# First weights whole with five loads in flight, and layer three's across product and mean of squares one unit later

## What is computed

```python
def hybrid_layer(x, mem, w_in, ...):              # layers one and two
    a_q, a_k, ..., m_q, m_z = split(x @ w_in)
    y_a = chunk_band_attention(...)               # 8 heads
    o_b = gla_chunk_recurrence(...)               # 4 heads, linear attention
    o_b = o_b * rsqrt(mean(square(o_b)) + RMS_EPS) * gla_norm_g
    mk, mv = split(mem @ w_mem_kv)
    y_m = memory_attention(m_q, mk, mv)           # 4 heads
    y = concat([y_a * silu(a_z), y_b * silu(b_z), y_m * silu(m_z)])
    return layer_norm(ALPHA * x + y @ w_out)

def second_block(x, ...):                         # layer three
    proj = rms_norm(x) @ w_in
    y_a = hgrn2_mixer(q, f, i, g)                 # 8 heads, linear attention, mean of squares per head
    y_b = fox_mixer(q, k, v, f_logit)             # 8 heads, causal softmax with decay
    merged = sigmoid(g_a) * (y_a @ w_up_a) + sigmoid(g_b) * (y_b @ w_up_b)
    x = x + rms_norm(merged @ w_o)
    gate, up = split(rms_norm(x) @ w_ffn_in)
    return x + rms_norm((silu(gate) * up) @ w_ffn_down)
```

## Time and profile before

| | us |
|---|---|
| median of three runs | 2255.04 (2253.93 to 2255.54) |
| the profiled execution's own time | 2254.65 |
| its span | 2252.8 |
| PE busy | 2241.2, 99% of the span |
| DVE busy | 1551.6, 69% |
| ACT busy | 1296.8, 58% |
| DMA | 460.04 MB, mean 204 GB/s |
| granted TensorE clock, mean | 0.999 |

### The profile page before, as it was taken

One profiled execution on the slowest core, in us unless ns is written; L12 is line 12 of the kernel. 1 busy time (PEld: TensorE's weight loads), 2 busy tenths in 40 slices (PEclk: granted clock), 3 DMA queues, 4 the chain that ended last, 5 costly groups with the idle time before them and its releaser, 6 DMA issues.

```text
span 2252.8 us, 35130 instructions
## 1 busy us (share of the span) xinstructions
PE 2241.2 (99%) x14045; PEld 2014.6 (89%) x14045; DVE 1551.6 (69%) x1756; ACT 1296.8 (58%) x1740; POOL 12.8 (1%) x18
## 2 busy tenths in 40 slices
PE   9999999999999999999999999999999999999998
PEld 8899998888999988889998999988999999998887
DVE  6576577775766777788787577866766766665555
ACT  6445576454555764666765467555655556554444
POOL 0000000000000000000000000000000000000000
PEclk9999999999999999999999999999999999999999
DMA  9655558676545684666565656685666666667664
GB/s 329 209 164 173 174 181 280 230 234 202 168 153 187 190 298 152 222 190 195 186 197 184 186 173 197 203 296 189 200 205 200 195 205 205 197 224 242 202 203 148
DMA packets 130532, 460.04 MB, mean 204 GB/s; under 512 B 13848, under 2 KB 20544, under 8 KB 128448
## 3 DMA queue, kind: packets, MB, share of 16 engines
q1 hardware_dynamic: 129376, 451.43, 61.9%
q0 software_dynamic: 848, 6.30, 0.8%
q10 hardware_dynamic: 144, 0.07, 0.0%
HBM read 449.35 MB, written 8.40 MB: 203 GB/s over the span
## 4 chain that ended last, share of the span: by engine, by line
PE 98%; DVE 1%; ACT 1%; DMA 0%; issue 0%; SPq 0%; DVEq 0%; ACTq 0%
PE banks L317 93%; PE banks L417 1%; PE banks L402 1%; PE banks L446 1%; PE banks L381 1%; PE banks L409 1%; DMA early<-in_kv_t 0%; DVE wl L650 0%; ACT wh L483 0%; PE banks L461 0%; PE banks L460 0%; PE banks L459 0%; PE banks L425 0%; DVE b L828 0%; DVE x_buf L923 0%
## 5 line engine op out<-in xcount | busy, mean ns | idle before, releaser
L650 DVE TENSOR_TENSOR wl<-raw,wh 128x1024 fp32r<-128x1024 f32 x774 | 941.1, 1223 | 476.9 <-ACT wh L483 474.5
L483 ACT ACTIVATE wh<-raw 128x1024 fp32r<-128x1024 f32 (+1 forms) x777 | 813.4, 1052 | 500.4 <-PE banks L317 437.2
L317 PE MATMUL banks<-xx,wh 128*128 128x512 f32 (+1 forms) x3760 | 858.5, 380 | 0.0
L317 PEld LDWEIGHTS banks<-xx,wh 128*128 128x128 f32 (+1 forms) x3760 | 688.2, 189 | 91.9 <-issue 1.0
L317 PEld LDWEIGHTS banks<-xx,wl 128*128 128x128 f32 x3712 | 455.2, 192 | 13.6
L317 PE MATMUL banks<-xx,wl 128*128 128x256 f32 x3712 | 464.6, 276 | 0.0
L317 PE MATMUL banks<-wh,xx 128*128 128x512 f32 x1504 | 360.2, 380 | 0.0
L317 PEld LDWEIGHTS banks<-wh,xx 128*128 128x128 f32 x1504 | 282.7, 189 | 39.4
L317 PE MATMUL banks<-wl,xx 128*128 128x512 f32 x752 | 196.1, 379 | 0.0
L317 PEld LDWEIGHTS banks<-wl,xx 128*128 128x128 f32 x752 | 142.1, 189 | 20.1
L317 PE MATMUL banks<-wh,yy 128*128 128x512 f32 x416 | 98.4, 379 | 0.0
(11 more groups left out here) (280 smaller groups left out, 1759.0 us busy)
## 6 DMA issues: line engine op xcount, KB each, us to landing
raw<-in_w_in_f SPq DMA_DIRECT2D x304, 512.0 KB, 3.6
raw<-in_w_ffn_f SPq DMA_DIRECT2D x160, 512.0 KB, 4.0
raw<-in_w_ffn_down SPq DMA_DIRECT2D x88, 512.0 KB, 4.3
raw<-in_w_in_t SPq DMA_DIRECT2D x80, 512.0 KB, 3.7
raw<-in_w_out_t SPq DMA_DIRECT2D x64, 512.0 KB, 4.8
raw<-in_w_o_t SPq DMA_DIRECT2D x32, 512.0 KB, 4.6
raw<-in_kv_f SPq DMA_DIRECT2D x16, 512.0 KB, 4.1
raw<-in_w_up_a_f SPq DMA_DIRECT2D x16, 512.0 KB, 3.5
```

Source lines behind the costliest of these rows:

```text
L317: return self.e.matmul(bank, stationary, moving, start=start, stop=stop, skip_group_check=True)
L483: self.e.activation(hi, source, ACT.Copy).then_inc(done.sem, 1)
L650: self.e.tensor_tensor(lo, source, hi.bitcast(f32), ALU.subtract).then_inc(done.sem, 1)
```

## The change

Three things are changed. The first weight is one unit again, the six `early` buffers are gone, and five loads are sent at the start; a load after that waits for its buffer's unit. In layer three the across product is written one unit later, and in all layers the mean of squares is. The mean of squares reads its columns in turn, and the root puts them back in order.

```diff
-        NR, NH, NE, AHEAD = 5, 4, 6, 2
+        NR, NH, AHEAD = 5, 4, 2
...
-        l_raw = lines(*(f"l_raw{n}" for n in range(NR + NE)))
+        l_raw = lines(*(f"l_raw{n}" for n in range(NR)))
...
-                    self.e.matmul(banks[6 + i], mean_r[:, :], a.hi[:, c], start=True, stop=False)
-                    j = self.e.matmul(banks[6 + i], mean_r[:, :], a.lo[:, c], start=False, stop=True)
+                    self.e.matmul(banks[6 + i], mean_r[:, :], in_turn(a.hi[:, c]), start=True, stop=False)
+                    j = self.e.matmul(banks[6 + i], mean_r[:, :], in_turn(a.lo[:, c]), start=False, stop=True)
...
-                    self.e.activation(r, banks[6 + i], ACT.Ln, bias=a.eps).then_inc(logged[i].sem, 1)
+                    self.e.activation(by_half(r), in_order(banks[6 + i]), ACT.Ln, bias=a.eps).then_inc(logged[i].sem, 1)
...
-                if early:
-                    plan(*among.pop(0))
-                    for kk in range(2):
-                        plan(w[0, :, 512 * kk:512 * kk + 512])
-                for u in range(early, n):
+                for u in range(n):
...
-            early = [at(f"early{n}", 48 + 4 * n, 1024) for n in range(NE)]
...
-                free = cut[n - NR] if n >= NE + NR else ()
-                sent.append(load(line, dst, src, *free))
+                free = cut[n - NR] if n >= NR else ()
+                sent.append(load(l_raw[n % NR], dst, src, *free))
...
-                if early:
-                    among_tok.append(cut[take(1)])
-                    for kk in range(2):
-                        unit_t(take(1), [(pr[t], act, t, kk, 0, kk == 0, False) for t in range(2)], among_tok[-1])
-                for k0 in range(2 * early, nk - 8 if late else nk, 2):
+                for k0 in range(0, nk - 8 if late else nk, 2):
...
                 if not a.both:
                     yield
+                    yield
                 tok = after(leveled)
                 x.across_halves(a, d, bank_free[6] + bank_free[7], tok)
...
                 x.split_squares(a, (sq[1], tok), h, l)
+                yield
                 yield
                 tok = after(meaned)
                 x.mean_squares(a, (h, l, co[1], t_exact), (), tok)
...
-            for n in range(NE + NR):
+            for n in range(NR):
                 send(n)
```

More of the change, by code:

```diff
@@ L1075, in send @@
                     return
-                src, (dst, line) = units[n][0], raw_of(n)
-                dst = dst[:, :]
+                src, dst = units[n][0], raw[n % NR][:, :]
                 if units[n][1] == "narrow":
@@ L1081, in send @@
                     dst = dst[:, 0:S * src.shape[1]].rearrange("p (a b) -> p a b", a=src.shape[1])
-                dst = dst[:, 0:src.shape[1]] if len(src.shape) == 2 else dst
-                free = cut[n - NR] if n >= NE + NR else ()
-                sent.append(load(line, dst, src, *free))
+                free = cut[n - NR] if n >= NR else ()
+                sent.append(load(l_raw[n % NR], dst, src, *free))
                 if n == 28:
@@ L1090, in split @@
                 src, hi, lo, free = units[n]
-                r = raw_of(n)[0][:, :]
+                r = raw[n % NR][:, :]
                 narrow = hi == "narrow"
@@ L1097, in split @@
                     hi, lo = place[n][0][:, :], place[n][1][:, :]
-                    if not narrow:
-                        hi, lo, r = (v[:, 0:src.shape[1]] for v in (hi, lo, r))
                 first, wide = hi, r
@@ L1225, in cols_t @@
                 ready = tuple(free) + bank_free[pr[0]] + bank_free[pr[1]]
-                early = among == "early"
-                if early:
-                    among_tok.append(cut[take(1)])
-                    for kk in range(2):
-                        unit_t(take(1), [(pr[t], act, t, kk, 0, kk == 0, False) for t in range(2)], among_tok[-1])
-                for k0 in range(2 * early, nk - 8 if late else nk, 2):
-                    if among and (k0 % 4 == 0 or early and k0 == 2):
+                for k0 in range(0, nk - 8 if late else nk, 2):
+                    if among and (k0 % 4 == 0 or among == "early" and k0 == 2):
                         among_tok.append(cut[take()])
```

## The result

| | before | after |
|---|---|---|
| median, the two measured together | 2254.01 (2253.46 to 2255.54, 11 runs) | 2259.56 (2258.31 to 2260.52, 11 runs) |
| ratio, 95% interval | | 1.0024 (1.0016 to 1.0031) |
| the profiled execution's own time | 2254.65 | 2259.41 |
| its span | 2252.8 | 2257.6 |
| granted TensorE clock, mean | 0.999 | 0.998 |

The changed kernel is 5.55 us slower, 0.25%. That is inside the range of the prediction, but not its likeliest case: it is a little over the 4.5 us that bound "no change" (the interval has the 0.2% in it, so on which side it lies is not settled), and, as the next rows show, it is the rival in which the clock falls.

A forecast was written before the change was run, and what follows sets the result against it. PE, busy 99% of 2252.8 us, was taken to bound the kernel. Start +0.1, across product -0.36, columns in turn -0.28 and mean of squares +4.1 summed to +3.56: median 2258.6 us, range 2256.2 to 2261.5.

The forecast's parts named there:

- likeliest case: Whole kernel: median 2258.6 us, 0.16% up and inside the 0.2% counted as no change; chance 0.55.
- the rival in which the clock falls: PE's new 4.7 us wait in layer three: clock drops, warm-up costs 1.9 us more, 2260.5 us; chance 0.22.
- The bound: Whole kernel: PE is busy 99% of 2252.8 us; moving waits could win under 3 us.
- Start, +0.1: First weight whole, five loads: second weight ready about as before; cost +0.1 us, bounds -0.1 and +0.5.
- The rival that rested on that stand: Start: PE idle 5.36 to 7.43, first weight's products at 1.2 GHz, 2.5 us lost, 2261.1 us; chance 0.11.
- Across product, -0.36: Layer three, first head group: one unit later covers DVE's product and removes PE's wait at L425; -0.36 us.
- In turn, -0.28: Sixteen mean-of-squares products: 0.215 us each instead of 0.233 when columns are read in turn; -0.28 us, bounds 0 and -0.3.
- Levels, 0: Layer three's level products (L446): no PE wait appears after the shift; 0 us, bounds -0.1 and +0.5.
- The stand, +4.1: Layer three, second group's mean of squares (L468): PE stands 4.68 us, old stall goes; net +4.1, bounds +3.6 and +4.5.
- PEclk whole in the slice of 1215 to 1235: Sign for the forecast: PE's granted clock stays full around its new wait at L468 in layer three.
- The sum: Whole kernel: 0.1 - 0.36 - 0.28 + 4.1 = +3.56 us, giving profile 2258.2 and median 2258.6.

The follow-up runs named there:

- e1: Kernel before with only the new start (first weight whole, five loads in flight): 2254.35 us, ratio 0.9999.
- e4: Kernel before with only the two added units (across product and mean of squares one unit later): 2260.21 us, ratio 1.0026.
- e6: Kernel before with only the across product of layer three's first group one unit later: 2258.56 us, ratio 1.0019.
- e10: Kernel before with only the columns of the mean of squares read in turn: 2254.23 us, ratio 1.0001.
- e3: Kernel before with five loads in flight at the start, first weight still in halves: 2254.48 us, ratio 1.0002.
- e5: Changed kernel with 19 unused products of the constant matrix on PE while it waits for the last mean of squares: 2257.37 us, ratio 1.0012.
- e8: Changed kernel whose walk no longer runs the lane to its end ahead of the second softmax group: 2252.57 us, ratio 0.9993.
- e9: Changed kernel with 8 unused products of the constant matrix on PE before the last mean of squares: 2257.67 us, ratio 1.0017.

## Why the prediction was right, and where not

- **The bound.** Right. PE is busy 99% and each of the losses and gains is one of PE's waits or durations. One wait was left out: 0.4 us at L381 (`z_buf`), in the body too. It is 0.4 in every run, so nothing hangs on it.
- **Start, +0.1.** Right in the median (e1: 0.0), and the argument for it too: the landing of the second weight ends the wait, not the first product. The detail was off: the first weight landed at 5.2 instead of 6.3, so PE began it at 6.32 instead of 7.43, and there was no stand of 2 us at the start; the 6.34 came from the late execution that had been profiled (with the same start e4, e6 and e10 rounded that piece at 5.4 to 5.5). The rival that rested on that stand did not come. In several traces, of the new start and of the old, the clock rose only at 6.6 to 7.2 us (e1, e3, e5, e6, e8, e9) instead of 4.3 to 5.6, and the medians of e1 and e3, which are among them, show no price. (The low clock at the start is read from the products of zeros, 0.43 us each until then and 0.23 after; the view of the grant shows 1.00 there.)
- **Across product, -0.36.** -0.45 in the trace. Right.
- **In turn, -0.28.** 0.06 us at three places and 0.04 at the fourth, 0.22 in the trace of e10: right in kind and a little less, below what the times of e10 can show. The cacheline rule of the Trainium skill (SBUF — State Buffer, "Door 1: The DMA port swizzle") is stated there for accesses to SBUF in general; applied to the moving operand of a matmul it would have each four take more than 0.93 us. Measured was 0.86, so for this operand the trace disagrees with it.
- **Levels, 0.** Right: no L446 among the waits.
- **The stand, +4.1.** Right: idle 4.44 us, predicted 4.2 to 4.6, and 4.1 net.
- **The clock.** Here the forecast went wrong. "PEclk whole in the slice of 1215 to 1235" was its stated mark, and it was 0.50 there for 6.8 us. The rival was named with its mechanism, but with a chance of 0.22, on the ground that the fall at the end came after some 5 us of standing and this stand was 4.7. A stand of 4.7 is much nearer to that 5 than to the 1.48 us that had been harmless; by the row it is nearest to, this rival was the likelier case. And the 5 us was one execution's: at the end of e5, where the last product ended at 2247.55, the clock was down after 2.1 us.

```profile
2247.60:2249.60 2.00, 0.00 (x0) 0.00 (x0) 1.70 (x4) 1.62 (x5) 0.47 (x1) 1.00 0.51 193
2249.70:2251.00 1.30, 0.00 (x0) 0.00 (x0) 1.30 (x3) 0.17 (x1) 1.05 (x1) 0.50 0.64 241
```

Over the twelve profiled executions this last stand lasted from 2.1 (e5) to 5.3 us (e3) before the clock fell, 5.2 in the kernel before. The price was somewhat small too: 2.3 us in the trace for 1.9. The 1.9 was the loss of the eleven sleeping products, 4.31 - 2.4; here 4.7 us of work ran at half speed, and in e4 6.2. The rule of the Trainium skill that was set beside it (TensorE: Matmul & The Clock Gate, "Part 1: The HAM clock gate"), that an array left idle goes back to half clock, agrees with the grant of 0.50 from 1224.2 to 1231.0.
- **The sum.** -0.45 - 0.22 + 4.1 + 2.3 = +5.7, measured +5.55. The forecast's +3.56 was 2.0 us short; the rival's +3.56 + 1.9 = +5.46 was right to 0.1. In absolute times it looks different, 2258.6 was 1.0 low and 2260.5 was 0.9 high, because both stand on the first median of before, 2255.04, and the runs beside the changed kernel gave 2254.01. So that the forecast comes within 1.0 us is in part luck. All eleven runs of the changed kernel lie above all ten of e5. Their mean granted clock is 0.997 or 0.998 in seven and 0.999 in the four fastest, which a short fall would leave at 0.999 as well; that the clock falls in each is inferred.

## What to carry to other kernels

A step moved later in a lane is free only as long as matmuls stand behind it: follow the lane to the place where it is run to its end, and count there what the shift has left uncovered, on the matmul engine and also in the order of the engines that feed it. A stand of TensorE of some microseconds in a busy kernel is priced as its length plus what the clock takes afterwards, which differs from one execution to the next; where it can't be removed, matmuls of a constant into a free bank keep the clock. And before an edit of a few tenths at the start is credited with anything, take several executions.

## What the runs showed of the hardware

- The clock fell in stands of 3.65 us (e6) and 4.4 us (after, e4), and held in one of 2.60 us (e9's profile). It fell after 3.65, 2.3 (after) and 3.8 us (e4) of standing, and at the end of the twelve kernels after 2.1 to 5.3 us. So the 2.60 us of e9 is no safe length; four of its ten times are longer, three of them with a lower mean clock.
- It then stayed at 1.2 GHz for 3.41 us (e6) and 6.83 us (after, e4). What this costs is about half of the part that falls on work: 3.4, 4.7 and 6.2 us of work, 1.7, 2.3 and 3.0 us lost.
- Nineteen products of a constant matrix, whose result nobody reads, kept the grant at 1.00 (e5) and were worth 2.3 us in the trace, 2.2 to 2.9 between medians.
- A moving operand of 512 columns is read faster in turn (columns 0, 256, 1, 257) than in order: 0.215 us a product against 0.233 (and 0.87 against 0.93 for four in e10).
- Five, ten or eleven loads in flight at the start made no difference that shows; from one execution to the next the landing of the second weight differs by 0.9 us.
